# Three sections of the adaLN modulation moved from layer 0's route into its attention, and the FFN columns with them

## The chip, the core and the metric

The kernel runs on one core of a Trainium2 chip. The metric is device microseconds (us) of one execution, as the median of several. Engines are named as the profile names them: PE (TensorE; its weight loads are listed apart as PEld), DVE (VectorE), ACT (ScalarE), POOL (GpSimd) and SP (SyncE, which only issues transfers here).

## The reference, cut to what matters

A backbone of two layers over 256 latent tokens and 256 context tokens, 1024 wide, in float32. Each layer scales and shifts its inputs by vectors that come from a conditioning vector:

```python
for l in range(DEPTH):
    mod = (silu_c @ w_mod[l] + b_mod[l])[:, None, :]      # (1024) @ (1024, 6144)
    modc = silu_cc @ w_mod[l] + b_mod[l]
    sh_a, sc_a, gt_a, sh_f, sc_f, gt_f = jnp.split(mod, 6, axis=-1)
    h = modln(x, g_attn[l], sh_a, sc_a)                   # rmsnorm * (1 + scale) + shift
    y, yc = token_mixers(h, hc, ...)                      # conv, neighbourhood, window attention
    x = x + gt_a * y
    h2 = modln(x, g_ffn[l], sh_f, sc_f)
    yt = hier_moe(toks, ...)                              # 32 experts, top 1 group, top 2 experts
    x = x + gt_f * yt
return rmsnorm(x, g_final)
```

The six parts of `mod` are called sections here, numbered 0 to 5 in that order: (l, 0) and (l, 1) shift and scale the attention's input, (l, 2) is its gate, (l, 3) and (l, 4) shift and scale the FFN's input, (l, 5) is the FFN's gate. None of them depends on the tokens, so each may be computed at any time before its use. Layer 1 leaves out the context tokens' outputs.

## The kernel before, in words

The program is written out by hand for each engine, with semaphores between them; the order of an engine's instructions is the order of its function calls. The stages of a layer are: input projection, attention, gates and branches, output projection with the residual, then what I call the **route** (FFN norm, router, top-2 choice, ranks of the tokens in their experts, selection matrices), then the experts in 16 pairs.

**Weights** stream through a ring of six slots of 1 MB. SP issues them in the order of `weight_stream` (L120 to L150); a transfer is issued when the chunk six places ahead of it has been released by its reader. A few chunks go around the ring into spare buffers (`load_spare`, L699).

**A section of the modulation** is four chunks of 1 MB in that stream (`mod`, L947). A chunk is eight matmuls of 32x256 in fp32 on PE, which the profile shows as 16 records. After the fourth chunk DVE adds the bias (`mod_add`, L1882), and for section 4 applies the norm's scale. Until that is done, the next section may not write the same PSUM bank, 7; the sections of the route have banks of their own (`ROUTE_BANK`).

**FFN columns** (`ffn_columns`, L976): 64 tiny matmuls of 32x2 (two sections, 32 each) turn sections 4 and 3 into per-partition columns, in banks 6 and 7; DVE copies them to `f_mul` and `f_add` (L1967). They are needed where the turned tokens leave PSUM, in the FFN norm.

**Attention** (`attention`, L1136 on PE, L2046 on DVE) goes over steps, one head for two blocks of 128 queries: 12 steps on latent queries, and in layer 0 another 12 on context queries. In the loop's turn s, PE does, if s is odd, the latent scores of step s+1 and the attend of steps s-3 and s-2 (L1132), then always the transposes of step s-1 (L1117), if s is odd the context scores of s+1 (L1102), and at last the chunks of the modulation that belong to step s-1 (`mod_chunks`). DVE adds the bias table to the scores (L2064), copies transposed probabilities (L2080), normalises (L2088) and finds the maximum (L2095); ACT does the exponentials (L1645) and the other copies.

Layer 0 computes three sections there, (0,2), (0,4), (0,3), one chunk in every second step, and layer 1 its own three in the same order, one chunk in each step. The route of layer 0 holds (0,5) ahead of the FFN columns, (1,1) ahead of the ranks and (1,0) behind them; the route of layer 1 holds (1,5).

**Route on PE** (L1497 to L1517): (l,5), FFN columns, `turn_h` (L960, transposes of the normalised tokens, tile by tile as DVE and ACT have scaled them at L1974 and L1557), `route` (router matmuls L1215, L1221), in layer 0 `turn_rows` (L1226, the tokens turned back for the selection matmuls; ACT copies them out twice, L1733), `ranks` (L1236, waits for DVE's choice at L2200), and `first_x` (L1309 to L1327), which gathers the tokens of the first experts and waits for DVE's selection matrix (L2239). Then the first expert pair's gate and up products start (L1263).

## Time and profile before

| | us |
|---|---|
| median of 3 runs | 1362.85 |
| lowest, highest | 1360.55, 1365.0 |
| profiled execution, its own time | 1366.03 |
| its span, first to last instruction | 1364.2 |
| PE busy | 1226.1 (90% of the span) |
| DVE busy | 649.0 (48%) |
| ACT busy | 438.0 (32%) |
| mean granted TensorE clock | 0.966 |

All durations below are from the profiled execution, whose own time is 3.2 us above the median of the runs. In the rows of the trace a line reads: start, duration (both us), engine, line of the program, operation, what it writes and reads, number of records, and in brackets how long the engine was idle before it and what ended that. "issue" there means that the engine waited for nothing that the profile shows. A row of the stretches reads: from and to, length, then busy time and number of records of PE, PEld, DVE, ACT and POOL, the granted TensorE clock (1.00 is 2.4 GHz, 0.50 is 1.2 GHz), the share of time in which the DMA engines were busy, and GB/s. A row of the chain reads: start, duration, engine and line, number of records.

### The profile page before, as it was taken

The numbers are of one execution on the slowest core, as the hardware profiler recorded it, in microseconds if no ns is written. First come the engines' busy times: TensorE is split into PE (matmuls) and PEld (weight loads), VectorE is DVE, ScalarE is ACT, GpSimd is POOL, SyncE is SP. The second block draws the span as 40 slices with busy tenths as digits, with TensorE's granted clock in tenths as the row PEclk, the third lists the DMA queues.
The fourth block names the chain that finished last, engine by engine and source line by source line (L and its number), as shares of the span: only waits on it lengthen the run. The fifth ranks groups of instructions, "written<-read, shape, count | busy, mean of one in ns | idle before, by whom it ended". The sixth has DMA issues, their size and how long they took to land.

```text
span 1364.2 us, 22180 instructions
## 1 busy us (share of the span) xinstructions
PE 1226.1 (90%) x8966; PEld 936.5 (69%) x8966; DVE 649.0 (48%) x1503; ACT 438.0 (32%) x1041; POOL 171.6 (13%) x212
## 2 busy tenths in 40 slices
PE   4999888899998989899999789998998868889986
PEld 2788754688887966666666469965998755555652
DVE  1544586464345463422221285667776545233334
ACT  3533366433334350010000364356665510000001
POOL 1810000111011300100000401001111200000001
PEclk9899899999999999999999889999998879999998
DMA  9994145423323279999999985248555859999995
GB/s 353 314 351 151 62 142 192 131 93 93 93 93 124 93 276 417 360 411 414 416 386 373 385 206 155 93 154 264 180 183 188 322 214 419 419 415 415 388 373 185
DMA packets 131831, 351.14 MB, mean 257 GB/s; under 512 B 23054, under 2 KB 84726, under 8 KB 108561
## 3 DMA queue, kind: packets, MB, share of 16 engines
q1 hardware_dynamic: 118144, 317.69, 63.1%
q0 software_dynamic: 12304, 30.37, 6.6%
q10 hardware_dynamic: 1280, 1.66, 0.4%
q8 instruction: 73, 1.20, 0.4%
q14 instruction: 30, 0.24, 0.1%
HBM read 330.53 MB, written 28.86 MB: 263 GB/s over the span
## 4 chain that ended last, share of the span: by engine, by line
PE 80%; DVE 8%; issue 4%; DMA 4%; ACT 2%; POOL 0%; SPq 0%; DVEq 0%; ACTq 0%; POOLq 0%
PE banks L1021 33%; PE banks L1263 16%; PE banks L1277 8%; PE banks L1255 6%; PE banks L1189 4%; PE banks L958 3%; PE banks L1117 2%; PE banks L1132 2%; PE banks L1102 2%; DMA expert_rows<-arena,rows_u 1%; DMA ring<-in_w_in 1%; DMA ring<-in_w_mod 1%; DMA ring<-in_w_e_up 1%; DVE arena L2352 1%; DVE att L2080 1%
## 5 line engine op out<-in xcount | busy, mean ns | idle before, releaser
L1994 DVE TENSOR_TENSOR w_lo_r<-ring,w_hi_r 128x256 fp32r<-128x256 f32 x480 | 222.7, 474 | 241.2 <-ACT w_hi_r L1618 240.1
L1618 ACT ACTIVATE w_hi_r<-ring 128x256 fp32r<-128x256 f32 x480 | 197.4, 416 | 304.6 <-PE banks L1021 254.9
L1263 PE MATMUL banks<-ring,arena 128*64 128x256 f32 x2016 | 233.8, 385 | 28.1 <-issue 11.5
L1021 PE MATMUL banks<-h_hi_r,w_hi_r 128*128 128x512 f32 (+1 forms) x640 | 221.8, 347 | 6.1 <-DVE h_lo_r L1938 4.7
L1263 PEld LDWEIGHTS banks<-ring,arena 128*64 128x64 f32 x2016 | 162.5, 138 | 89.0 <-issue 37.4
L1021 PE MATMUL banks<-h_lo_r,w_hi_r 128*128 128x512 f32 (+1 forms) x640 | 220.2, 344 | 0.0
L1021 PE MATMUL banks<-h_hi_r,w_lo_r 128*128 128x512 f32 (+1 forms) x640 | 220.1, 344 | 0.0
L1021 PEld LDWEIGHTS banks<-h_hi_r,w_hi_r 128*128 128x128 f32 x640 | 122.9, 192 | 22.5 <-ACT arena L1588 4.8
L1021 PEld LDWEIGHTS banks<-h_lo_r,w_hi_r 128*128 128x128 f32 x640 | 123.0, 192 | 13.8
L1021 PEld LDWEIGHTS banks<-h_hi_r,w_lo_r 128*128 128x128 f32 x640 | 122.8, 192 | 13.8
L1277 PE MATMUL banks<-ring,att 128*64 128x512 f32 x424 | 119.3, 604 | 14.1 <-DVE att L2369 7.4
L1741 ACT ACTIVATE arena<-banks 128x256 f32<-128x256 f32 x32 | 12.3, 384 | 294.3 <-PE banks L1263 294.3
L1021 PE MATMUL banks<-w_hi_r,h_hi_r 128*128 128x256 f32 x320 | 94.7, 296 | 9.4 <-DVE w_lo_r L1994 9.1
L2362 DVE TENSOR_TENSOR arena<-arena,banks 128x256 f32<-128x256 f32 x32 | 13.5, 421 | 184.6 <-PE banks L1263 184.6
L1021 PE MATMUL banks<-w_hi_r,h_lo_r 128*128 128x256 f32 x320 | 92.8, 290 | 0.0
L1021 PE MATMUL banks<-w_lo_r,h_hi_r 128*128 128x256 f32 x320 | 92.7, 290 | 0.0
L1277 PEld LDWEIGHTS banks<-ring,att 128*64 128x64 f32 x424 | 36.9, 138 | 73.9 <-issue 71.4
L1255 PE MATMUL banks<-att_r,h_hi_r 128*128 128x256 f32 x336 | 85.5, 293 | 0.0
L898 POOL DMA_INDIRECT expert_rows<-arena,rows_u x30 | 29.5, 984 | 419.8 <-ACT arena L1750 166.7
L1255 PE MATMUL banks<-att_r,h_lo_r 128*128 128x256 f32 x336 | 81.3, 281 | 0.0
L1255 PEld LDWEIGHTS banks<-att_r,h_hi_r 128*128 128x128 f32 x336 | 63.4, 189 | 16.7 <-issue 16.7
L1021 PEld LDWEIGHTS banks<-w_hi_r,h_hi_r 128*128 128x128 f32 x320 | 63.6, 199 | 12.4 <-DVE w_lo_r L1994 11.2
(269 smaller groups left out, 1726.3 us busy)
## 6 DMA issues: line engine op xcount, KB each, us to landing
ring<-in_w_e_gate SPq DMA_DIRECT2D x64, 1024.0 KB, 8.7
ring<-in_w_e_up SPq DMA_DIRECT2D x62, 1024.0 KB, 9.3
ring<-in_w_e_down SPq DMA_DIRECT2D x53, 1024.0 KB, 9.3
ring<-in_w_mod SPq DMA_DIRECT2D x48, 1024.0 KB, 6.6
ring<-in_w_in SPq DMA_DIRECT2D x38, 1024.0 KB, 5.5
expert_rows<-att POOLq DMA_DIRECT2D x23, 512.0 KB, 20.3
ring<-in_w_o SPq DMA_DIRECT2D x8, 1024.0 KB, 5.1
ring<-in_w_branch SPq DMA_DIRECT2D x8, 640.0 KB, 4.5
```

The lines of the kernel that those rows point to most:

```text
L898: pool.indirect_dma_start(out=yd, out_offset=bass.IndirectOffsetOnAxis(ap=rows_u[:, p:p + 1], axis=0), in_=y_sb[n % 2], in_offset=None, bo ...
L958: ins = mm(banks[32 * q:32 * q + 32, mod_bank(l, sec), 0:CW], cond32[:, 2 * j2 + k, :], w[:, k, q * CW:(q + 1) * CW], start=j2 == 0 and k ...
L1021: ins = mm(out_ap, a, b, start=k == 0 and p_ == 0, stop=k == KD - 1 and p_ == 2)
L1102: ins = mm(banks[:, 2 * e + part, b * SEQ:(b + 1) * SEQ], arena[p0:p0 + HD, tn, q0 + b * P:q0 + (b + 1) * P], arena[p0:p0 + HD, kt, part * ...
L1117: ins = turn(banks[:, 4 + b, q * P:(q + 1) * P], S[s % 3][:, b, q * P:(q + 1) * P], ident)
L1132: ins = mm(banks[HD * e:HD * e + HD, O_BANK, 0:2 * P], vals[:, t0 + q, v0:v0 + HD], PT[e][:, q, :], start=q == 0, stop=q == n - 1)
L1189: ins = mm(outs[half], wt, y, start=k == BRANCH[b][0] and p_ == 0, stop=k == BRANCH[b][-1] and p_ == 2)
L1255: ins = mm(out, h[:, tt, k * P:(k + 1) * P], picked[:, tt, :], start=tt == 0 and h is th_hi, stop=tt == QT[l] - 1 and h is th_lo)
L1263: ins = mm(banks[e * CAP:(e + 1) * CAP, bank, 0:DE], x[:, k, e * CAP:(e + 1) * CAP], w[:, k * DE:(k + 1) * DE], start=k == 0, stop=k == KD ...
L1277: ins = mm(banks[e * CAP:(e + 1) * CAP, Y_BANK + half, :], rows[:, k, e * CAP:(e + 1) * CAP], w[k][:, half * 512:half * 512 + 512], start= ...
L1618: fn(w_hi[:, u % AHEAD, :, :], chunk(key)[:, q * KU:(q + 1) * KU, :], ACT.Copy).then_inc(w_hi_ready, 1)
L1994: v.tensor_tensor(w_lo[:, u % AHEAD, :, :], chunk(key)[:, q * KU:(q + 1) * KU, :], w_hi[:, u % AHEAD, :, :].bitcast(F32), ALU.subtract).th ...
```

## The change

All six sections that layer 0 used to compute from its attention on are computed in its attention: the order is (0,4), (0,3), (0,2), (0,5), (1,1), (1,0). `MOD_STEP` gives each chunk its step: one in each of steps 0 to 7, none in 8 and 9, two in step 10, then one in each step but for two in step 17. Layer 1 has (1,4), (1,3), (1,2) with chunks in steps 0 to 7, and two each in steps 9 and 10. In step 8 of either layer PE computes the FFN columns, into bank 7 beside the sections' 256 columns, and DVE copies them out in its turn for that step. Layer 1's (1,5) stays in the route, now in bank 7 and behind all of the residual's updates, not three quarters of them. The token tiles of `turn_rows` go to other banks, so that three tiles are turned ahead of the ranks, and one behind. The stream of weights follows the same order. The core of the diff:

```diff
@@ -114,3 +114,2 @@
-MOD_IN = [[(0, 2), (0, 4), (0, 3)], [(1, 2), (1, 4), (1, 3)]]
-MOD_ROUTE = [[(0, 5), (1, 1), (1, 0)], [(1, 5)]]
-MODS = [(0, 1), (0, 0)] + MOD_IN[0] + MOD_ROUTE[0] + MOD_IN[1] + MOD_ROUTE[1]
+MOD_IN = [[(0, 4), (0, 3), (0, 2), (0, 5), (1, 1), (1, 0)], [(1, 4), (1, 3), (1, 2)]]
+MODS = [(0, 1), (0, 0)] + MOD_IN[0] + MOD_IN[1] + [(1, 5)]
@@ -140 +139,2 @@
-        out += [("mod", k, 4 * sec + j) for k, sec in MOD_ROUTE[l] for j in range(4)]
+        if l:
+            out += [("mod", 1, 4 * 5 + j) for j in range(4)]
@@ -561,6 +561,4 @@
-        ROW_BANKS = [(3, 0), (4, 5), (3, 0), (4, 5)]
-        ROUTE_BANK = {(0, 5): 0, (1, 1): 7, (1, 0): 6, (1, 5): 0}
-
-        def mod_bank(l, sec):
-
-            return ROUTE_BANK.get((l, sec), MOD_BANK)
+        ROW_BANKS = [(3, 0), (4, 5), (6, 7), (3, 0)]
+        F_COL = {4: 256, 3: 256 + 2 * KD}
+        F_COL_STEP = [8, 8]
+        MOD_STEP = [[0, 1, 2, 3, 4, 5, 6, 7] + [10 + 14 * q // 16 for q in range(16)], list(range(8)) + [9, 9, 10, 10]]
@@ -570,2 +568 @@
-            n = 4 * len(MOD_IN[l])
-            return range(n * s // len(STEPS[l]), n * (s + 1) // len(STEPS[l]))
+            return [q for q, at in enumerate(MOD_STEP[l]) if at == s]
@@ -719 +716 @@
-                    sp.wait_ge(f_cols_done, 4)
+                    sp.wait_ge(f_cols_done, 2)
@@ -952 +949 @@
-                if n and j2 == 0 and (l, sec) not in ROUTE_BANK:
+                if n and j2 == 0:
@@ -953,0 +951,3 @@
+                for m in range(DEPTH):
+                    if j2 == 0 and (l, sec) == MOD_IN[m][2]:
+                        pe.wait_ge(f_col_ready, 2 * (m + 1))
@@ -958 +958 @@
-                        ins = mm(banks[32 * q:32 * q + 32, mod_bank(l, sec), 0:CW], cond32[:, 2 * j2 + k, :],
+                        ins = mm(banks[32 * q:32 * q + 32, MOD_BANK, 0:CW], cond32[:, 2 * j2 + k, :],
@@ -978,2 +978,2 @@
-                for sec, bank in ((4, 6), (3, 7)):
-                    pe.wait_ge(mod_out, MOD_AT[(l, sec)] + 1)
+                for sec in (4, 3):
+                    pe.wait_ge(mod_out, MOD_AT[MOD_IN[l][1]] + 1)
@@ -980,0 +981 @@
+                        at = F_COL[sec] + 2 * k
@@ -982 +983 @@
-                            ins = mm(banks[32 * j:32 * j + 32, bank, 2 * k:2 * k + 2], modr[:, l, sec, k::KD],
+                            ins = mm(banks[32 * j:32 * j + 32, MOD_BANK, at:at + 2], modr[:, l, sec, k::KD],
@@ -984 +985 @@
-                    ins.then_inc(f_cols_done, 1)
+                ins.then_inc(f_cols_done, 1)
@@ -1153,0 +1155,4 @@
+                        if s - 1 == F_COL_STEP[l]:
+                            ffn_columns(l)
+                pe.wait_ge(f_col_ready, 2 * (l + 1))
+                pe.wait_ge(mod_out, 2 + len(MOD_IN[0]) + l * len(MOD_IN[1]))
@@ -1228,2 +1233,2 @@
-                    if tt >= 2:
-                        pe.wait_ge(th_hi_ready, tt - 1)
+                    if tt == 3:
+                        pe.wait_ge(th_hi_ready, 1)
@@ -1314 +1319 @@
-                    pe.wait_ge(th_hi_ready, 3)
+                    pe.wait_ge(th_hi_ready, 4)
@@ -1317,3 +1321,0 @@
-                    for key in MOD_ROUTE[l][1:]:
-                        if k == ROUTE_BANK[key]:
-                            pe.wait_ge(mod_out, MOD_AT[key] + 1)
@@ -1497,3 +1498,0 @@
-                pe.wait_ge(upd_ready, 4 * QT0[l] + 3 * QT[l])
-                for j2 in range(4):
-                    mod(*MOD_ROUTE[l][0], j2)
@@ -1501,2 +1500,4 @@
-                ffn_columns(l)
-                pe.wait_ge(mod_out, MOD_AT[MOD_ROUTE[l][0]] + 1)
+                if l:
+                    for j2 in range(4):
+                        mod(1, 5, j2)
+                    pe.wait_ge(mod_out, MOD_AT[(1, 5)] + 1)
@@ -1506,4 +1507 @@
-                    turn_rows((0, 1))
-                for k, sec in MOD_ROUTE[l][1:2]:
-                    for j2 in range(4):
-                        mod(k, sec, j2)
+                    turn_rows((0, 1, 2))
@@ -1512,4 +1510 @@
-                    turn_rows((2, 3))
-                for k, sec in MOD_ROUTE[l][2:]:
-                    for j2 in range(4):
-                        mod(k, sec, j2)
+                    turn_rows((3,))
@@ -1889 +1884 @@
-                ins = v.tensor_tensor(dst, banks[:, mod_bank(l, sec), 0:CW], dst, ALU.add)
+                ins = v.tensor_tensor(dst, banks[:, MOD_BANK, 0:CW], dst, ALU.add)
@@ -1961 +1956,2 @@
-                mod_add(*MOD_ROUTE[l][0])
+                if l:
+                    mod_add(1, 5)
@@ -1964,5 +1959,0 @@
-                    if tt == nt // 2:
-                        for n, (dst, bank) in enumerate(((f_mul, 6), (f_add, 7))):
-                            dve.wait_ge(f_cols_done, 2 * l + n + 1)
-                            v.tensor_copy(dst[:, :, :], banks[:, bank, 0:2 * KD].rearrange("p (k s) -> p k s", s=2))\
-                                .then_inc(f_col_ready, 1)
@@ -2073,0 +2065,6 @@
+                        if s - 2 == F_COL_STEP[l]:
+                            dve.wait_ge(f_cols_done, l + 1)
+                            for sec, dst in ((4, f_mul), (3, f_add)):
+                                at = F_COL[sec]
+                                v.tensor_copy(dst[:, :, :], banks[:, MOD_BANK, at:at + 2 * KD].rearrange("p (k s) -> p k s", s=2))\
+                                    .then_inc(f_col_ready, 1)
@@ -2545,2 +2541,0 @@
-                if l == 0:
-                    mod_add(*MOD_ROUTE[0][1])
@@ -2549,3 +2544 @@
-                    rest_rows(0, range(2))
-                    mod_add(*MOD_ROUTE[0][2])
-                    rest_rows(0, range(2, 4))
+                    rest_rows(0, range(4))
```

How the order of the instructions changes, at three places on PE. In the rows, L1102 or L1103 are scores, L1117 or L1118 transposes of probabilities, L1132 or L1133 the attend matmuls, L958 a chunk of the modulation, L982 or L983 the FFN columns, L972 `turn_h`.

PE in layer 0's attention, turns 9 and 10 of the loop, before:

```order
L1117 MATMUL banks<-consts,att 128x128 [waits pt_act,pt_dve,p_ready]
L1117 MATMUL banks<-consts,att 128x128 x7
L1102 MATMUL banks<-arena 128x256 [waits s_act]
L1102 MATMUL banks<-arena 128x256 x3
L1117 MATMUL banks<-consts,att 128x128 [waits pt_act,pt_dve,p_ready]
L1117 MATMUL banks<-consts,att 128x128 x7
L958 MATMUL banks<-ring,cond 32x256 [waits loaded4,mod_out]
L958 MATMUL banks<-ring,cond 32x256 x7
```

and as changed:

```order
L1118 MATMUL banks<-consts,att 128x128 [waits pt_act,pt_dve,p_ready]
L1118 MATMUL banks<-consts,att 128x128 x7
L1103 MATMUL banks<-arena 128x256 [waits s_act]
L1103 MATMUL banks<-arena 128x256 x3
L983 MATMUL banks<-consts,modr 32x2 [waits mod_out]
L983 MATMUL banks<-consts,modr 32x2 x31
L983 MATMUL banks<-consts,modr 32x2 [waits mod_out]
L983 MATMUL banks<-consts,modr 32x2 x31
L1118 MATMUL banks<-consts,att 128x128 [waits pt_act,pt_dve,p_ready]
L1118 MATMUL banks<-consts,att 128x128 x7
```

The columns stand between the scores and the next transposes, and turn 10 has no chunk; two chunks follow in turn 11 and one in turn 12.

PE at the start of layer 0's route, before:

```order
L958 MATMUL banks<-ring,cond 32x256 [waits loaded5]
L958 MATMUL banks<-ring,cond 32x256 x7
L982 MATMUL banks<-consts,modr 32x2 [waits mod_out,upd_ready]
L982 MATMUL banks<-consts,modr 32x2 x31
L982 MATMUL banks<-consts,modr 32x2 [waits mod_out]
L982 MATMUL banks<-consts,modr 32x2 x31
L972 MATMUL banks<-consts,arena 128x128 [waits f_x_dve,f_x_act,f_col_ready,mod_out]
L972 MATMUL banks<-consts,arena 128x128 x7
```

and as changed, right behind the last matmul of the output projection:

```order
L1022 MATMUL banks<-w_lo_r,h_hi_r 128x256
L972 MATMUL banks<-consts,arena 128x128 [waits f_x_dve,f_x_act,f_col_ready,upd_ready]
L972 MATMUL banks<-consts,arena 128x128 x7
L972 MATMUL banks<-consts,arena 128x128 [waits f_x_act,f_x_dve]
L972 MATMUL banks<-consts,arena 128x128 x7
```

Nothing stands between the projection and `turn_h` any more; likewise the eight chunks around the ranks are gone.

PE at the start of layer 1's route as changed (before, it reads like layer 0's, with the four chunks first):

```order
L958 MATMUL banks<-ring,cond 32x256 [waits loaded5]
L958 MATMUL banks<-ring,cond 32x256 x7
L958 MATMUL banks<-ring,cond 32x256 [waits loaded0]
L958 MATMUL banks<-ring,cond 32x256 x7
L958 MATMUL banks<-ring,cond 32x256 [waits loaded1]
L958 MATMUL banks<-ring,cond 32x256 x7
L972 MATMUL banks<-consts,arena 128x128 [waits f_x_dve,f_x_act,f_col_ready,mod_out]
L972 MATMUL banks<-consts,arena 128x128 x7
```

The chunks stay, and the 64 matmuls of the columns no longer stand between them and `turn_h`.

## Rows read from the trace of the kernel before

**Rows 1.** The profile's page, parts 1, 3 and 4.

```profile
PE 1226.1 (90%) x8966; PEld 936.5 (69%) x8966; DVE 649.0 (48%) x1503; ACT 438.0 (32%) x1041; POOL 171.6 (13%) x212
...
q8 instruction: 73, 1.20, 0.4%
...
PE 80%; DVE 8%; issue 4%; DMA 4%; ACT 2%; POOL 0%; SPq 0%; DVEq 0%; ACTq 0%; POOLq 0%
```

**Rows 2.** Stretches: layer 0's attention, route and experts.

```profile
162.00:247.00 85.00, 69.47 (x602) 43.61 (x604) 65.28 (x160) 56.63 (x158) 2.49 (x4) 0.96 0.46 149
...
476.60:519.50 42.90, 37.52 (x500) 28.82 (x499) 26.71 (x92) 19.97 (x42) 3.68 (x6) 0.96 0.76 297
524.90:762.00 237.10, 223.46 (x1802) 153.38 (x1800) 59.53 (x158) 21.63 (x31) 20.15 (x23) 1.00 0.99 396
```

**Rows 3.** Chain of waits, attend matmuls: two of layer 0's, three of layer 1's.

```profile
188.48 1.95 PE banks L1132 x16
196.59 1.95 PE banks L1132 x16
...
916.12 1.95 PE banks L1132 x16
924.24 1.88 PE banks L1132 x16
932.91 1.95 PE banks L1132 x16
```

**Rows 4.** Timeline of PE in layer 0's attention, turn 12's transposes.

```profile
209.44 1.09 PE L1117 MATMUL banks<-consts,att 128*128 128x128 f32 x8 [0.77 <-DVE att L2088]
```

**Rows 5.** Timeline of layer 0's route, from the projection's end.

```profile
476.75 3.66 PE L958 MATMUL banks<-ring,cond 128*32 128x256 f32 x64
...
480.23 1.97 PE L982 MATMUL banks<-consts,modr 128*32 128x2 f32 x118
...
480.53 2.56 ACT L1557 ACTIVATE arena<-X,stat 128x512 f32<-128x512 f32 x4 [0.24 <-DVE stat L1960]
...
483.83 0.35 PE L982 MATMUL banks<-consts,modr 128*32 128x2 f32 x10 [1.64 <-issue]
...
484.49 3.81 PE L972 MATMUL banks<-consts,arena 128*128 128x128 f32 x32 [0.31 <-DVE f_add L1967]
```

**Rows 6.** Timeline of layer 0's route, from the choice to the first gather.

```profile
500.77 0.16 DVE L2202 TENSOR_TENSOR rt<-top_e 128x4 f32<-128x4 f32 x1
...
502.47 0.49 PE L1239 MATMUL banks<-att,consts 128*128 128x128 f32 x2
502.62 0.42 DVE L1889 TENSOR_TENSOR modr<-banks,modr 128x256 f32<-128x256 f32 x1 [1.68 <-PE banks L958]
...
507.79 1.67 DVE L2239 SCALAR_TENSOR_TENSOR att_r<-consts,sel_slot,att 128x256 fp32r<-128x256 f32 x4
...
509.74 4.02 PE L1323 MATMUL banks<-att_r,h_hi_r 128*128 128x256 f32 x32
```

**Rows 7.** Timeline of layer 1's route: the last update to `turn_h`.

```profile
1076.39 0.78 DVE L2156 TENSOR_TENSOR att<-banks,gate_t 128x256 f32<-128x256 f32 x2 [1.47 <-PE banks L1021]
...
1080.12 2.10 PE L982 MATMUL banks<-consts,modr 128*32 128x2 f32 x128
...
1080.71 0.73 DVE L1971 TENSOR_SCALAR arena<-X,stat 128x512 f32<-128x512 f32 x1
...
1082.56 1.21 PE L972 MATMUL banks<-consts,arena 128*128 128x128 f32 x8 [0.34 <-issue]
...
1088.04 1.97 PE L972 MATMUL banks<-consts,arena 128*128 128x128 f32 x8 [4.27 <-issue]
```

**Rows 8.** DMA queues from 1080 to 1088 us: packets, MB, share of time.

```profile
q8 instruction: 1, 0.02, 0.8%
```

**Rows 9.** Stretches: the first gathers of both layers.

```profile
509.70:517.50 7.80, 7.80 (x68) 7.57 (x64) 5.29 (x7) 1.01 (x1) 0.00 (x0) 1.00 1.01 415
...
1104.70:1110.30 5.60, 5.60 (x26) 5.60 (x27) 0.00 (x0) 0.00 (x0) 0.00 (x0) 0.50 0.09 34
```

## The prediction

> **What bounds the kernel now.** I read the profile's page first, then stretches by stage, then the chain of waits and the timeline where the change touches it. PE is busy for 90% of the span and holds 80% of the chain that ended last [rows 1]. Not so in each stage. In layer 0's attention PE is busy for 69.5 of 85 us and DVE for 65.3: neither is full, and the turns run at the pace of the chain between them [rows 2]. In layer 0's route PE is busy for 37.5 of 42.9 us, much of it with the modulation that is to move. In layer 0's experts the DMA engines are busy for 0.99 of the time at 396 GB/s [rows 2]: that stage starts when the first gate product can start, and its length is set by transfers behind it. So two things count: how much later attention ends, and how much earlier each layer's first gate product starts.
>
> 0.3%, or 4.1 us, is about what a measurement of this kernel can tell from no change.
>
> **Layer 0's attention, +3.0 us.** A chunk costs PE 3.66 / 4 = 0.92 us [rows 5]. Twelve more make 11.0 us, the columns 2.1 us: 13.1 us if nothing hid them. The trace has a direct comparison for the latent steps. Layer 0 has a chunk in every second step, and two steps take 196.59 - 188.48 = 8.11 us; layer 1 has one in every step, and two steps take 924.24 - 916.12 = 8.12 us [rows 3]. The second chunk is free there: PE fills a gap that it has ahead of the even turn's transposes, 0.77 us waiting for DVE [rows 4]. But where DVE does section 4's double addition, two steps of layer 1 take 932.91 - 924.24 = 8.67 us, 0.55 more [rows 3]. That addition moves from layer 0's light context steps into its latent ones: +0.5.
> The columns take 2.0 to 2.1 us of PE [rows 5, 7] in that gap of 0.77, so the next transposes come 1.3 us late; DVE has a copy to do for them and its own slack of some tenths: +0.9. It could be 0, or 2.1 and the stall of 1.64 that stands inside layer 0's columns now [rows 5], 3.7 in all.
> Step 10's two chunks are 1.83 us against 0.77: +1.1, bounds 0 and 1.8.
> In the context steps PE and DVE both have more room; of some seven added chunks I take +0.5, bounds 0 and 6.4 (none hidden).
> Sum +3.0, ends 0 and 13.1, both unlikely; +1 to +6 is what I keep. Twelve more transfers in this stage are 12.6 MB, 30 us at 415 GB/s [rows 9], on top of a share of 0.46 over 85 us [rows 2]: about 0.8, still free, and each is issued six chunks ahead. Cost nothing; if gates came late, the projection behind would show it. POOL now writes layer 1's gate row at the end of attention, ahead of its casts for the merge; these are first needed by the branch matmuls, behind three gate chunks, so nothing.
>
> **Layer 0's route, -1.5 us**, in three terms.
> The start: `turn_h` starts at 484.49, released by DVE's copy of the columns, whose matmuls stood still for 1.64 us [rows 5]. Without them it waits for the scaled tiles: ACT does four in 2.56 us from 480.53, so the first is there at 481.2 and the last at 483.1. At full clock the last tile is turned 0.95 us later, at 484.1, against 488.3 now: -4.2. But PE, which the modulation and the columns keep at work now, then stands idle from 476.6 to 481.2. Layer 1 shows what follows: after 4.27 us of idleness a tile takes 1.97 us, not 0.95 [rows 5, 7]. Four such from 481.2 end at 489.1: +0.8. I take the middle, -1.7, as the clock comes back within the stage.
> The ranks: the choice is ready at 500.93, but (1,1)'s chunks hold PE until 502.47, and its addition holds DVE for 0.42 us [rows 6]. Both go: -1.9. ACT's copies of the four tiles stay hidden, since three tiles are now turned ahead of the ranks.
> The first gather: it starts at 509.74, 0.28 us after the selection matrix (507.79 + 1.67), and takes 7.8 us at a clock of 1.00 [rows 6, 9], with (1,0) right ahead of it on PE. That work is gone; what is left is idle. Layer 1's gather, after idleness, runs 26 records in 5.6 us at 0.50, 0.215 us each; layer 0's 68 in 7.8, 0.115 each [rows 9]. If 4 to 5 us run so: +2.1; ends 0 and +7.8 (all of it at half rate).
> Sum -1.7 - 1.9 + 2.1 = -1.5; ends -6.1 and +6.7.
> What does not come back as time is the 12 MB: the ring holds six chunks, which in either order have landed before the first gate product. Layer 1 shows that state: 0.09 of DMA just ahead of it [rows 9].
>
> **Layer 1's attention, 0.** The columns come in (+0.9, bounds 0 and 3.7), and the last chunk and its addition leave the tail, where PE's 0.92 and DVE's 0.42 lie between the last transposes and the last attend (bounds 0 and -1.4): -0.9.
>
> **Layer 1's route, -5.5 us.** Tile 0 is turned at 1082.56, tile 1 only at 1088.04: PE stood still for 4.27 us with no wait that the profile shows, and the tile ends at 1090.0 [rows 7]. I put this down to PE running out of instructions. The instruction queue moved one packet in those 8 us, at a time when data transfers filled the engines [rows 8]. On the page 73 packets carry 1.20 MB, and PE's two rows count 17,932 instructions [rows 1]; if most packets are PE's, one holds about 250. The columns are 128 matmul records and as many weight loads, 256 in 2.1 us: they eat a whole packet while the next is on its way. Layer 0's columns show the same, 1.64 us [rows 5]. Moved into the attention, they no longer stand where the expert weights fill the queues.
> Then: (1,5) waits for the last update, at 1076.39 + 0.78 = 1077.2, takes 3.66 and ends at 1080.8; the addition ends near 1081.4; DVE's two scalings of 0.73 us make tile 1 ready near 1082.8 [rows 7]. Turned at 1.97 us it ends at 1084.9, at 0.95 at 1083.8, against 1090.0: -5.1 or -6.2. I take -5.5. If the stall stays, (1,5) later by some tenths and the columns gone leave about -1.2.
> By the Trainium skill, "Runtime: NRT & Kernel Launch", section "Instruction fetch mechanics", the next block is fetched while the current one is executed and crossing a block's end is mostly hidden; by that rule the 4.27 us would be something else and would stay, and the sum would be near 0. No row here decides between the two; the idle times behind both sets of columns speak for my reading.
>
> **Sum.** +3.0 - 1.5 + 0 - 5.5 = -4.0. Against the profiled execution that is 1366.0 - 4.0 = 1362.0; its own time lies 3.2 above the median, so against the median it is 1362.85 - 4.0 = 1358.8 us.
>
> **Rivals.**
> *The stall stays or moves.* The 4.27 us are not the columns', or they come back in the attention, which has the same 256 instructions in 2.1 us. For it: no row proves the cause. Against: two places, both at columns. -4.0 + 4.3 = +0.3: 1363.2 us. Chance 0.18, all but 0.02 of it within 0.3%.
> *Layer 0's route at half clock*, the slower side. The modulation was what kept PE at 2.4 GHz between DVE's pieces; without it `turn_h` ends 0.8 later, not 1.7 earlier (+2.5), and the whole gather runs at half rate (+7.8, not +2.1: +5.7), with 2 us in the router's matmuls. It decides once the idle stretches ahead of `turn_h` and of the gather, about 4.6 and 3 us, each bring the clock down, and it stays there, as over 5.6 us of layer 1's gather [rows 9]. -4.0 + 2.5 + 5.7 + 2 = +6.2: 1369.1 us. Against: in layer 0 PE has twice as much work in each burst. Chance 0.12.
> *More is won.* The clock holds in layer 0's route (-2.5 and -2.1), or the 12 MB that no longer queue there let the expert weights land sooner: -4.0 - 4.6 = -8.6, 1354.2 us. Chance 0.20.
> *The attention pays for the chunks in full* would be +13.1 and end slower too; rows 3 speak against it, and I fold it into the range.
>
> **How the numbers follow.** The forecast has 0.50, with a range of its own of 1355 to 1363; its centre lies at the bound of 0.3% (1358.8), so half of it is faster (0.26) and half within (0.24). With the rivals: faster 0.26 + 0.20 = 0.46, within 0.24 + 0.16 = 0.40, slower 0.12 + 0.02 = 0.14. For 8 in 10 the range must reach most of the way to the outer cases: 1351 to 1367.
>
> **What would show it.** In layer 1's route, `turn_h`'s second tile right behind the first, with no idle time of 4 us; the first gate product 5 to 6 us nearer to the end of the projection. In layer 0, `turn_h` some 4.6 us behind the last projection matmul, the ranks right behind DVE's choice, and a clock of 0.50 over part of the gather. In attention, latent pairs of steps still near 8.1 us but for those with section 4's addition, the columns and step 10. The prediction is wrong if layer 0's attention grows by more than 6 us, if an idle time of 2 us or more stands within or behind the columns in attention, or if the experts of layer 0 take another time than 237 us from their first gate product's end on.

## The result, and the profile after

The changed kernel takes 1387.17 us (median of 4 runs, 1378.04 to 1389.42) against 1361.70 us (4 runs, 1360.53 to 1365.00) on the same chip: a ratio of 1.017 with a 95% interval of 1.0121 to 1.022. The forecast was 1358.8 with a range up to 1367. The direction was wrong, and none of the rivals had this size.

The page of the changed kernel looks almost like [rows 1]: PE is as busy as before, with 15 us more of busy time.

```profile
PE 1241.2 (90%) x8966; PEld 946.5 (68%) x8966; DVE 648.7 (47%) x1503; ACT 439.2 (32%) x1041; POOL 171.7 (12%) x212
...
q8 instruction: 73, 1.20, 0.3%
```

The stretches that answer to [rows 2]: layer 0's attention, route and experts.

```profile
162.00:259.00 97.00, 85.49 (x926) 51.65 (x928) 65.85 (x164) 56.78 (x158) 2.32 (x4) 0.93 0.69 243
490.30:533.40 43.10, 30.29 (x176) 26.96 (x176) 25.12 (x86) 19.97 (x42) 3.36 (x6) 0.76 0.20 74
538.80:776.00 237.20, 222.46 (x1766) 153.24 (x1762) 59.31 (x156) 21.67 (x31) 20.09 (x23) 0.99 0.98 388
```

Attention is 12 us longer; PE has 16 us more work in it than before, and the granted clock is 0.93, not 0.96. The route lost 7 us of PE's work and not a microsecond of time: its clock went from 0.96 to 0.76.

Cut at the same events in each trace (us; the last column is a second profile of the unchanged kernel, the run `before_again`):

| from - to | before | after | difference | before again |
|---|---|---|---|---|
| start - layer 0's first attend | 172.37 | 172.30 | -0.07 | 172.83 |
| - its last attend | 74.43 | 86.19 | **+11.76** | 74.41 |
| - output projection's end | 230.02 | 231.78 | +1.76 | 228.53 |
| - first gate product (route) | 42.66 | 43.17 | +0.51 | 43.32 |
| - last down products (experts) | 254.24 | 257.24 | +3.00 | 259.91 |
| - layer 1's first attend | 134.20 | 134.35 | +0.15 | 132.73 |
| - its last attend | 41.03 | 48.38 | **+7.35** | 41.04 |
| - output projection's end | 127.76 | 128.51 | +0.75 | 126.83 |
| - ranks | 23.16 | 18.79 | **-4.37** | 22.06 |
| - end | 264.29 | 264.56 | +0.27 | 264.71 |

(The spans differ by 21.1 us, 1364.2 and 1385.3; the profiled run of before, at 1366.03, was 4.3 us above the median of its four runs, hence 25.5 between the medians.) The two attentions are the loss, 19.1 us. In the unchanged kernel their times repeat to 0.02 us from one profile to the next, while the experts' differ by 5.7 us; that stage keeps the DMA engines busy for 0.98 to 0.99 of the time, and its +3.00 says nothing about the change. In the changed kernel the attentions repeat less well. Four of the experiments below (`columns_repeated`, `long_products`, `kept_warm`, `warm_short`) leave its attention code as it is, and in these four profiles and its own layer 0's attention takes 86.2 to 88.9 us and layer 1's 46.6 to 48.5.

Inside layer 0's attention, from the timeline of PE and DVE:

```profile
199.18 1.09 PE L1118 MATMUL banks<-consts,att 128*128 128x128 f32 x8
201.27 1.90 PE L983 MATMUL banks<-consts,modr 128*32 128x2 f32 x108
203.93 0.54 PE L983 MATMUL banks<-consts,modr 128*32 128x2 f32 x20 [0.77 <-issue]
204.57 0.17 DVE L2069 COPY f_mul<-banks 128x16 f32<-128x16 f32 x1 [4.46 <-PE banks L983]
204.75 0.68 DVE L2077 COPY att<-banks 128x512 f32<-128x512 f32 x1
205.53 0.88 DVE L2085 TENSOR_SCALAR att<-att,rsum 128x512 f32<-128x512 f32 x2
206.47 1.97 PE L1118 MATMUL banks<-consts,att 128*128 128x128 f32 x8 [2.00 <-DVE att L2085]
...
223.81 0.42 DVE L1884 TENSOR_TENSOR modr<-banks,modr 128x256 f32<-128x256 f32 x1 [3.57 <-PE banks L958]
225.34 0.66 PE L1118 MATMUL banks<-consts,att 128*128 128x128 f32 x4 [1.67 <-DVE att L2085]
...
236.83 0.42 DVE L1884 TENSOR_TENSOR modr<-banks,modr 128x256 f32<-128x256 f32 x1 [2.70 <-PE banks L958]
```

This is what I did not see. DVE waits for the columns, or for a section's last chunk, at the head of a turn; the copy of P, the normalisation and the maximum stand behind that wait. The columns belong to step 8, so PE does them in turn 9. An odd turn is the full one: attend, transposes, scores, and only then the chunk. DVE stands for 4.46 us, its work comes late, PE waits 2.00 us for the normalised rows, and behind that the granted clock is 0.50: a turn's transposes take 1.97 us instead of 1.09. The last chunks of sections 2 and 5 fall on steps 12 and 16, also even, with idle times of 3.57 and 2.70. Before the change every section's last chunk stood at an odd step.

Layer 1's attention shows the same at its columns, with no stall inside them, and again in its last pair of steps, where section 2's last chunk falls on the even step 10:

```profile
954.00 2.15 PE L983 MATMUL banks<-consts,modr 128*32 128x2 f32 x128
956.29 0.17 DVE L2069 COPY f_mul<-banks 128x16 f32<-128x16 f32 x1 [3.45 <-PE banks L983]
958.19 1.97 PE L1118 MATMUL banks<-consts,att 128*128 128x128 f32 x8 [2.03 <-DVE att L2085]
...
968.59 0.42 DVE L1884 TENSOR_TENSOR modr<-banks,modr 128x256 f32<-128x256 f32 x1 [5.52 <-PE banks L958]
970.66 1.97 PE L1118 MATMUL banks<-consts,att 128*128 128x128 f32 x8 [2.13 <-DVE att L2085]
```

The routes. Layer 0's, then layer 1's (they answer to [rows 5, 6] and [rows 7]):

```profile
494.82 6.00 PE L972 MATMUL banks<-consts,arena 128*128 128x128 f32 x32 [4.55 <-ACT arena L1552]
...
513.50 0.80 PE L1244 MATMUL banks<-att,consts 128*128 128x128 f32 x2 [2.71 <-DVE att L2197]
...
521.08 6.61 PE L1325 MATMUL banks<-att_r,h_hi_r 128*128 128x256 f32 x32 [2.20 <-DVE att_r L2236]
...
1107.44 1.94 PE L972 MATMUL banks<-consts,arena 128*128 128x128 f32 x16 [1.34 <-ACT arena L1549]
```

In layer 0, `turn_h` begins 4.55 us behind the projection (forecast 4.6), but its 32 turns take 6.00 us instead of 3.81, and the gather's first half 6.61 instead of 4.02. In layer 1 the 16 turns run without the stall of 4.27 us. A slow `turn_h` is not new in itself: in the second profile of the unchanged kernel layer 0's takes 5.43 us, at no cost, since (1,1)'s chunks still stand between it and the ranks (18.05 us from its start to theirs, 17.98 in the first profile).

### The profile page after: what moved, and what is told of

Same layout as the page of the kernel before. It is cut to its first block and busy times, and to the rows that moved or that the text cites. A ratio compares the mean times of both kernels' runs of the same rounds, so it can differ in the third digit from the quotient of the medians.

```text
span 1385.3 us, 22186 instructions
## 1 busy us (share of the span) xinstructions
PE 1241.2 (90%) x8966; PEld 946.5 (68%) x8966; DVE 648.7 (47%) x1503; ACT 439.2 (32%) x1041; POOL 171.7 (12%) x212
## 5 line engine op out<-in xcount | busy, mean ns | idle before, releaser
L1268 PE MATMUL banks<-ring,arena 128*64 128x256 f32 x2016 | 237.9, 390 | 27.3 <-issue 10.6
L1260 PEld LDWEIGHTS banks<-att_r,h_hi_r 128*128 128x128 f32 x336 | 63.4, 189 | 16.7 <-issue 16.7
```

The lines of the kernel that those rows point to most:

```text
L1260: ins = mm(out, h[:, tt, k * P:(k + 1) * P], picked[:, tt, :], start=tt == 0 and h is th_hi, stop=tt == QT[l] - 1 and h is th_lo)
L1268: ins = mm(banks[e * CAP:(e + 1) * CAP, bank, 0:DE], x[:, k, e * CAP:(e + 1) * CAP], w[:, k * DE:(k + 1) * DE], start=k == 0, stop=k == KD ...
```

## The experiments

**Theory A**, formed from these traces: the place of DVE's wait, head of turn behind PE's full turn, costs the attention. **Theory B**, the rival: the chunks and columns are simply more work than PE's gaps hold.

### Four edits of the order

`columns_step_9`:

```diff
-F_COL_STEP = [8, 8]
-MOD_STEP = [..., list(range(8)) + [9, 9, 10, 10]]
+F_COL_STEP = [9, 9]
+MOD_STEP = [..., list(range(8)) + [10, 10, 11, 11]]
```

> The changed kernel with the FFN columns one step later, at the odd step 9 in both layers (layer 1's last section goes from steps 9, 9, 10, 10 to 10, 10, 11, 11, since it must come behind them). Theory A, the place of DVE's wait: at an even step PE does a chunk or the columns in its odd turn, behind attend, transposes and scores, and DVE waits for them at the head of its own turn with the copy of P, the normalisation and the maximum behind it; at an odd step PE does them right behind the transposes and DVE waits for little. Then the pair of steps with the columns falls from 12.4 us to about 9 and the next from 9.4 to about 8.5 in layer 0, and in layer 1 from 13.6 and 9.8 to about 9.5 and 8.3: 4 and 5 us less, 1387 to 1378. Theory B, PE's own work: 2.1 us of columns and the chunks are simply more than PE's gaps hold, wherever they stand, and an idle clock does the rest; then the pairs only trade places and the sum of each layer's attention stays within 2 us: 1385 to 1389.

`last_chunks_odd` (layer 0's chunks behind step 9):

```diff
-10 10 11 12 | 13 14 15 16 | 17 17 18 19 | 20 21 22 23
+10 10 11 13 | 14 15 16 17 | 18 18 19 19 | 20 21 22 23
```

> The changed kernel with layer 0's chunks behind step 9 on other steps, so that the last chunk of section 2 is at step 13 and that of section 5 at step 17, both odd (they were at 12 and 16); the columns stay at step 8 and the number of chunks is the same. Theory A (place of DVE's wait): the pairs of steps that cost 1.86 and 2.42 us more than before the change are back at 5.6 to 6.4 us, 4 us less in layer 0's attention, 1383 us. Theory B (the chunks' own time on PE): no change in the sum of the context pairs beyond 1 us, 1386 to 1388.

`columns_9_and_odd`: both, with 10, 11, 12, 13 for the first section.

> Both edits together, and step 10 with one chunk instead of two. Theory A: layer 0's attention ends 2 to 4 us later than before the change (it was 11.7), layer 1's takes 1 to 2 us more (it was 7.4), so 13 to 14 us less than the changed kernel, and some of the 1.9 us by which the projection behind attention grew and of the 2.8 us in layer 0's experts may go too: 1368 to 1374 us. Theory B: 1383 to 1388 us.

`adds_late` (DVE alone; `for_mod` holds the additions and column copies of step s - 2, as they were):

```diff
+def for_mod(l, s, late):
+    if s >= 2 and (s % 2 == 0) == late:
+        ...
 ...
-if s >= 2:
-    ...
+for_mod(l, s, False)
 if 0 <= s - 2 < n:
     ...
         v.tensor_reduce(negmax[:, s % 3, :], buf[:, :, 0:w], AX.X, ALU.max, negate=True).then_inc(max_ready, 1)
+for_mod(l, s, True)
```

> The changed kernel with PE's order untouched. Only DVE's waits and the work behind them (a section's addition, the two copies of the columns) that fall into its even turns, those for a chunk or columns of an even step, stand at the end of the turn, behind the copy of P, the normalisation and the maximum. The direct test of theory A: PE does the same work at the same places, so under theory B nothing changes (1386 to 1388). Under theory A the idle times of DVE of 4.46, 3.57 and 2.70 us ahead of the copy and the additions go, the pair with the columns falls from 12.4 to about 9.5 us, the context pairs by 1.5 to 2.4 us each, in layer 1 the pair of 13.6 to about 10: 10 to 13 us less, 1374 to 1377.

Measured, with the kernel before at 1362.77 us (19 runs) on the same chip: `columns_step_9` 1375.39 (5 runs), ratio 1.0081 (1.0049 to 1.0113); `last_chunks_odd` 1388.13 (4 runs), 1.0184 (1.0143 to 1.0225); `columns_9_and_odd` 1378.22 (9 runs), 1.0111 (1.0082 to 1.014); `adds_late` 1371.27 (10 runs), 1.0065 (1.0037 to 1.0093).

The distance from one attend to the next is the plainest measure, since each ends a pair of steps. It is worked out from the attends' starts in the timelines (us; pairs 4 to 11 are layer 0's, the last two layer 1's; the last three kernels come below; a last digit can be off by one through rounding):

| pair | before | after | step 9 | odd | late | columns_only | shifted | quarters |
|---|---|---|---|---|---|---|---|---|
| 4 | 8.05 | 12.38 | 9.02 | 13.09 | 9.18 | 8.96 | 8.30 | 8.06 |
| 5 | 7.09 | 9.38 | 9.49 | 9.37 | 10.19 | 8.66 | 9.88 | 7.54 |
| 6 | 6.44 | 8.30 | 8.30 | 6.44 | 6.44 | 6.44 | 6.44 | 6.98 |
| 7 | 6.20 | 5.58 | 5.57 | 5.57 | 5.57 | 5.58 | 6.27 | 5.58 |
| 8 | 5.58 | 8.00 | 8.00 | 6.27 | 6.33 | 5.58 | 5.58 | 5.58 |
| 9 | 5.58 | 6.27 | 6.27 | 8.00 | 6.28 | 5.58 | 5.58 | 5.58 |
| 10 | 5.58 | 5.58 | 5.59 | 5.58 | 5.59 | 5.75 | 6.74 | 6.21 |
| 11 | 5.68 | 5.68 | 5.67 | 7.37 | 6.73 | 5.09 | 5.09 | 5.09 |
| L1 columns | 8.05 | 13.62 | 9.02 | 12.64 | 8.94 | 8.30 | 8.30, 8.06 | 8.05, 8.06 |
| L1 last | 7.98 | 9.75 | 11.70 | 8.91 | 7.32 | 10.47 | 7.30 | 7.98 |

Theory A holds where it is tested alone. In `adds_late` PE's order is untouched and the pair with the columns goes from 12.38 to 9.18, the pairs of steps 12 and 16 from 8.30 and 8.00 to 6.44 and 6.33, layer 1's from 13.62 to 8.94. In its trace DVE's idle time ahead of the columns' copy is 0.96 us, not 4.46, and ahead of the additions of steps 12 and 16 there is none:

```profile
203.63 0.17 DVE L2041 COPY f_mul<-banks 128x16 f32<-128x16 f32 x1 [0.96 <-PE banks L983]
...
205.93 3.68 PE L1133 MATMUL banks<-att,arena 128*64 128x256 f32 x16 [0.84 <-DVE att L2080]
```

From the first attend to the last, layer 0's attention takes 81.31 us instead of 86.19 and layer 1's 41.26 instead of 48.38, both outside what the changed attention shows from one execution to another. The median, 1371.27, lies below the 1374 to 1377 of the forecast, 8.5 us above the kernel before on its chip, where the changed kernel stood 25.5 above; theory B had no change. The span is 16.7 us shorter, 12.0 of it in the two attentions; the rest is spread over the other stages.

Theory A is not all of layer 0's loss, though. Layer 1's attention is back at its old length (41.03), layer 0's is still 6.9 us above its 74.43. The largest part is pair 5, 3.1 us, which rose from 9.38 to 10.19 (7.09 before the change): its attend runs at half rate, 3.68 us instead of 1.95, and step 10's two chunks are in it. The pair with the columns keeps 1.1 us, three context pairs keep 0.7 to 1.1 each; one is 0.6 shorter than before the change.

`columns_step_9` also met its forecast at the columns (9.02); the pair behind them did not fall (9.49, forecast 8.5), and it lost some of the gain in layer 1's last pair (11.70), where four chunks had gone.

`last_chunks_odd` missed its 1383 us. The two pairs that it was made for fell as forecast (6.44, 6.27), and two others rose as much. The timeline of the pair that went from 6.27 to 8.00:

```profile
242.98 1.93 PE L958 MATMUL banks<-ring,cond 128*32 128x256 f32 x32
...
244.84 0.66 PE L1118 MATMUL banks<-consts,att 128*128 128x128 f32 x4
...
245.43 1.93 PE L958 MATMUL banks<-ring,cond 128*32 128x256 f32 x32
...
247.50 0.42 DVE L1884 TENSOR_TENSOR modr<-banks,modr 128x256 f32<-128x256 f32 x1 [3.03 <-PE banks L958]
```

The section now ends at step 19, odd, but with two chunks in each of two turns, and DVE waits 3.03 us for them. So an odd step is no rule in itself: here the wait is as long as all of PE's work up to the chunk that DVE waits for. The last pair (7.37) is another thing. DVE stands there behind a split of weights that ACT had to wait for:

```profile
258.65 1.33 ACT L1613 ACTIVATE w_hi_r<-ring 128x256 fp32r<-128x256 f32 x4 [1.99 <-DMA ring<-in_w_in]
259.10 1.43 DVE L1985 TENSOR_TENSOR w_lo_r<-ring,w_hi_r 128x256 fp32r<-128x256 f32 x4 [2.12 <-ACT w_hi_r L1613]
```

I read it as their ring slots coming free later, with the chunks; no run tests that alone. I had priced it at nothing.

`columns_9_and_odd` missed too, 1378 us for 1368 to 1374: the same two pairs rose (8.00 and 7.23), pair 5 stayed at 8.72 and layer 1's last at 10.39. Layer 1's pairs in `last_chunks_odd` (12.64 and 8.91) are no gain of its edit: `columns_repeated` and `long_products` have 12.66 and 8.91 with the changed kernel's attention.

### The stall in layer 1's route: instructions, or something else

Both edits stand in layer 1's route of the changed kernel, between section 5's chunks and `turn_h`.

`columns_repeated`:

```diff
+for sec in (4, 3):
+    for k in range(KD):
+        for j in range(4):
+            ins = mm(banks[32 * j:32 * j + 32, 5, 2 * k:2 * k + 2], modr[:, 1, sec, k::KD], ident[:, 32 * j:32 * j + 2], ...)
```

> The changed kernel with layer 1's 128 column matmuls done a second time in its route, behind section 5's chunks and ahead of turn_h, into a bank that nobody reads: the same number of PE instructions at the place where they stood before the change (the last spare load waits for them, as it did then). Theory C, PE runs out of instructions: a stall of 3 to 5 us with no wait that the profile shows comes back within or behind them, and the run is 5 to 7 us longer than the changed kernel's. Theory D, the stall of 4.27 us was something else that the change happened to remove: the repeated columns take their 2.0 to 2.1 us and turn_h follows without an idle time of over 1 us.

`long_products`:

```diff
+for _ in range(12):
+    ins = mm(banks[:, 5, 0:384], ident, consts[:, 0:384], ...)
```

> The control for the repeated columns: at the same place 12 products of 128x384 instead, which hold PE for about as long (by the rows with 512 columns, 0.23 us each, 12 x 0.17 = 2.05 us) with 12 matmuls and 12 weight loads at most instead of 256 instructions; the last spare load waits for them in the same way. Under theory C no idle time of over 1 us behind them; under D the same as the run with repeated columns. If both runs show the stall, it comes of PE's time or of the spare load's wait, not of the count.

The timelines of PE, first with the columns repeated, then with the long products:

```profile
1103.41 2.10 PE L1506 MATMUL banks<-consts,modr 128*32 128x2 f32 x128
1105.44 0.98 PE L972 MATMUL banks<-consts,arena 128*128 128x128 f32 x7
1109.22 2.08 PE L972 MATMUL banks<-consts,arena 128*128 128x128 f32 x9 [2.80 <-issue]
```

```profile
1108.78 8.01 PE L1504 MATMUL banks<-consts 128*128 128x384 f32 x24
1116.63 1.91 PE L972 MATMUL banks<-consts,arena 128*128 128x128 f32 x16
```

With the columns' 128 products and 128 weight loads done once more (records; the program has 64 of each) the stall is back, 2.80 us after the seventh turn; with few records there is none. Three flaws. The long products took 8.01 us, not 2.05, since each is two records of 0.33 us here, so this control is no equal in time. The stall came out a little under the 3 to 5 us expected. And the run's time, 1387.24 us (one run), is that of the changed kernel, not 5 to 7 us more: from the projection's end to the ranks layer 1 takes 21.73 us instead of 18.79, and other stages of this one execution were shorter by as much in sum. The second profile of the unchanged kernel shows how far the stall's size varies, at the same place (behind the eighth turn, where [rows 7] have 4.27):

```profile
1085.44 1.06 PE L972 MATMUL banks<-consts,arena 128*128 128x128 f32 x8 [0.34 <-issue]
1088.99 1.97 PE L972 MATMUL banks<-consts,arena 128*128 128x128 f32 x8 [2.48 <-issue]
```

The columns in attention bear it out. With the columns at step 8, six of seven traces have an idle time "issue" behind the same 108th record of layer 0's columns, 0.22 to 2.10 us long; with the columns at step 9, two of two have none. With the columns in halves at steps 8 and 9 (below), two of three have it behind the 100th (0.40 and 0.97), and `kept_warm` has 0.64 within layer 1's.

Counting settles the place. Put all of PE's entries in a trace in order of time, products, weight loads and semaphore instructions alike, and count those ahead of the first product behind the stall. They are 2753 in each of the eight traces with a stall in layer 0's attention, 5825 in layer 0's route in both profiles of the unchanged kernel, 12768 in layer 1's attention (`kept_warm`), 15072 in layer 1's route in both profiles of the unchanged kernel, and 15327 in `columns_repeated`. 2753 and 5825 lie 12 x 256 apart, 12768 and 15072 lie 9 x 256 apart, and 15327 is one short of another 256; between the two layers there is an offset of 31, for which I have no account. So all of these stalls stand where another 256 entries are through, which is what running out of instructions at the end of a block would look like; the fetch of a block is not itself in these rows. In `columns_step_9` number 2753 falls within the columns too, and nothing stops there: the 256 entries before it took 6.4 us, against 2.6 to 5.7 us ahead of all the stalls. A short block does not suffice for one: `shifted` passes such places after 5.7 and 3.2 us without a stall, `columns_repeated` one after 4.7.

The length is another matter. It does not follow the load of the DMA engines alone: they were busy for the whole of the stalls of 4.27, 2.48 and 2.80 us, and for 0.02 of the time in the one of 2.10 us (`long_products`, layer 0). The program decides the place; what decides the length is open.

### The cold clock in layer 0's route

`kept_warm` and `warm_short` put products that nobody reads into the gap ahead of layer 0's `turn_h`, 24 of them and 6:

```diff
+for _ in range(24):    # 6 in warm_short
+    mm(banks[:, 5, 0:384], ident, consts[:, 0:384], ...)
```

> The changed kernel with 24 products of 128x384 (24 x 0.17 = 4.1 us) in layer 0's route, behind the wait for the last update and ahead of turn_h, where PE stands idle for 4.55 us; what they compute is read by nobody. Theory E, the idle stretches that the change left in layer 0's route cost time by the clock: turn_h's 32 turns take 3.8 us instead of 6.0, the router and the choice come 1.5 to 2 us earlier, the gather is as slow as before since PE is idle again ahead of it: 1385 us against 1387. If the tiles or DVE set the pace of turn_h anyway, nothing changes (0 to +0.5 us).

> The changed kernel with 6 products of 128x384 in layer 0's gap of 4.55 us ahead of turn_h instead of 24. In the run with 24 they took 15.75 us, 0.66 each (two passes of 0.33), so 6 take 3.9 us and fit. Theory E (the clock that falls in the idle stretches left in the route costs time there): turn_h in 3.8 us instead of 6.0, the ranks 16.6 us behind turn_h's start as in the run with 24, instead of 18.7; 1.5 to 2 us less than the changed kernel, 1385. If the gain is lost again at the gather, which stays cold behind its own idle time, 0 to 1 us.

The 24 took 15.75 us instead of 4.1, by the same wrong price: 1391.83 us (ratio 1.0214, 1.0168 to 1.0261). The 6 fit into the gap: 1382.00 us, ratio 1.0149 (1.0127 to 1.0172), the kernel before at 1362.4 (17 runs). From the timeline of PE in `warm_short`:

```profile
488.40 4.14 PE L1506 MATMUL banks<-consts 128*128 128x384 f32 x12 [0.52 <-DVE att L2156]
492.44 3.81 PE L972 MATMUL banks<-consts,arena 128*128 128x128 f32 x32
...
508.86 0.49 PE L1244 MATMUL banks<-att,consts 128*128 128x128 f32 x2 [1.04 <-DVE att L2200]
...
515.37 6.41 PE L1325 MATMUL banks<-att_r,h_hi_r 128*128 128x256 f32 x32 [3.63 <-DVE att_r L2239]
```

`turn_h` is back at 3.81 us, the ranks' first products at 0.49 instead of 0.80, and the route at 39.6 us (527.50 - 487.88) instead of 43.17: 3.6 us from 4.1 us of work for nothing. The gather, behind an idle time of its own, stays at 6.41. This gain is read in the stage: `turn_h`'s start to the ranks is 18.4 to 18.8 us in the eight profiles with that gap left empty, 16.42 and 16.62 in the two with it filled. The ratios of the two kernels, 1.0149 and 1.017, do not differ clearly, their intervals overlap.

### The change cut down

`columns_only`: layer 0's sections go back to the route, the columns stay in attention, in halves at steps 8 and 9, DVE's even turns as in `adds_late`.

> Only the columns are moved: layer 0's three sections stay in its route, as in the kernel before, and each layer's columns stand in its attention, section 4's at step 8 and section 3's at step 9, with DVE's copies at turn 11; DVE's additions for even steps stand behind its maximum, and the sections' last chunks in the context steps are at odd steps. Theory A: layer 1's route is 4.7 us shorter, layer 0's 2 to 3, layer 0's attention 2 to 4 us longer (section 4's addition 0.6, the columns 1, half a clock behind them 1 to 2), layer 1's 2 to 3: 1357 to 1363 us, against 1362.8 before. Theory B (the attention pays for whatever is put there at its full price or more): 1366 us or more. If the 2.3 to 3.9 us by which layer 0's experts are longer in all runs with its sections in attention come of the sections, they are gone here; if of the columns, they stay.

1367.34 us (10 runs) against 1363.67 (13 runs), ratio 1.0034 (1.0009 to 1.0058): 4 us above the forecast range of 1357 to 1363 and in what the expectation had given to theory B (1366 or more), though its profiled span was 1362.7 against the 1364.2 and 1366.4 of the two profiles of before. The pairs show where: layer 1's last pair, with four chunks in its two steps, takes 10.47 us instead of 7.98. Layer 1's stretch to the ranks is 17.77 us (-5.4), layer 0's route 39.81 (-2.9) at a clock of 0.96; the attentions took 2.2 and 2.7 us more than before (first to last attend, 76.64 and 43.76).

`split_late` keeps all that the change moves, with the columns in halves, DVE's even turns late, and layer 0's chunks behind step 9 at 10 to 17 and 18 18 19 20 21 22 23 23:

> All that the changed kernel moves stays moved, but with its three faults taken out as the runs so far show them: DVE's additions of even steps behind its maximum, the columns in two halves at steps 8 and 9, never two chunks in a latent step of layer 0 and the last chunks at odd steps (13, 17, 20, 23). Theory A: layer 0's attention 3 to 6 us longer than before the change, layer 1's 3 to 4 (its last two steps carry four chunks), routes 5 us shorter, layer 0's experts 2.5 longer: 1366 to 1371 us, better than the changed kernel by 16 or more and still not better than the kernel before.

1375.89 us (4 runs), ratio 1.0101 (1.008 to 1.0122), above the forecast range. The last pair of layer 0, with three chunks in its two steps, took 8.85 us.

`shifted`, from `columns_only`:

```diff
-MOD_IN = [[(0, 4), (0, 3), (0, 2)], [(1, 4), (1, 3), (1, 2)]]
+MOD_IN = [[(0, 4), (0, 3), (0, 2), (1, 4)], [(1, 3), (1, 2)]]
-F_COL_AT: layer 1 at 8 and 9; its chunks at 0 to 7, 10 10 11 11
+F_COL_AT: layer 1 at 4 and 5; its chunks at 0 1 2 3, 6 7 8 9
```

> The kernel with only the columns moved, and layer 1's section 4 computed in layer 0's context steps (chunks at 12 to 15; section 2's layer 0 at 12 to 15, this one at 18 to 21), so that layer 1's attention carries two sections: chunks at steps 0 to 3 and 6 to 9, the columns in two halves at 4 and 5, none in the last two steps. Expected against the kernel with only the columns moved: layer 1's attention 2 to 3 us shorter (its last pair of steps 8.0 instead of 10.5, no double addition of 0.6), layer 0's 0.5 to 1.5 us longer in the context steps (a wait of 0.7 us per section, as the pair of 6.27 against 5.58 shows), 1 to 2 us less in all: 1364 to 1367 us by its 1367.3, level with the kernel before within 0.3%.

1360.93 us (12 runs) against 1362.4 (17 runs), ratio 0.9999 (0.9977 to 1.0021): no difference from the kernel before, and 3 us below the 1364 to 1367 expected. Layer 1's attention is down to 40.13 us, layer 0's is at 78.87. What was left there was above all pair 5, 9.88 us: the attend behind the columns ran at half rate.

`quarters` (from `shifted`), and `before_again`, the unchanged kernel:

```diff
-F_COL_AT[0] = {8: [(4, 0, KD)], 9: [(3, 0, KD)]}
+F_COL_AT[0] = {8: [(4, 0, 4)], 9: [(4, 4, KD)], 10: [(3, 0, 4)], 11: [(3, 4, KD)]}
+F_COL_AT[1]: the same at 4 to 7; layer 1's last section at 8 9 10 11
+layer 0's context chunks at 12 13 13 15, 17 18 19 21
```

> The shifted kernel with each layer's columns in quarters of 32 products, one behind each of four steps' turns (8 to 11 in layer 0, 4 to 7 in layer 1), the sections' last chunks in layer 0's context steps each behind a step without a chunk (chunks at 12, 13, 13, 15 and 17, 18, 19, 21), layer 1's last section at steps 8 to 11. If the clock falls behind the columns because 64 or more of these small products in a row leave PE little to do, the attend behind them runs at full rate again (1.95 us, not 3.68) and layer 0's pair of 9.88 us is back at 7.1 to 7.6; the context pairs of 6.27 and 6.74 are back at 5.6 to 5.8: 3 to 4 us less in layer 0's attention, 1357 to 1359 us, 0.3% better than the kernel before. If it is the idle time of 1.04 us ahead of the attend that brings the clock down, that pair stays above 9 us: 1359 to 1362.

> The kernel before, unchanged, for a second profile of it: the stage times on which the comparisons rest, from another execution. In eight profiles of changed kernels layer 0's experts take 2.3 to 7 us more from the first gate product to the last down product of the loop than the 254.2 us of the one profile of before. If that is the change, this profile shows 254.2 again within 0.5 us; if it is how its transfers happen to fall, it differs by 2 us or more. The attention's pairs of steps should agree within 0.1 us, the stall in layer 1's route (4.27 us) within 1.

In `shifted`, and in `quarters`, the attend that follows the last columns:

```profile
206.53 3.68 PE L1141 MATMUL banks<-att,arena 128*64 128x256 f32 x16 [1.04 <-DVE att L2095]
```

```profile
213.43 0.67 PE L990 MATMUL banks<-consts,modr 128*32 128x2 f32 x32
...
215.15 1.95 PE L1141 MATMUL banks<-att,arena 128*64 128x256 f32 x16 [1.04 <-DVE att L2095]
```

The idle time ahead of the attend is the same 1.04 us, and the attend takes 3.68 us in one and 1.95 in the other. So it is not that idle time alone: with the small products spread over four steps instead of two the clock held. Nor is it the small products alone. In layer 1 of `shifted` the same two runs of them are followed by scores in place of the idle time, and the attend takes 1.95 us:

```profile
922.67 1.17 PE L990 MATMUL banks<-consts,modr 128*32 128x2 f32 x64
923.77 1.13 PE L1111 MATMUL banks<-arena 64*128 64x256 f32 x8
924.88 1.95 PE L1141 MATMUL banks<-att,arena 128*64 128x256 f32 x16
```

In these rows it takes both. Pair 5 fell to 7.54, and layer 0's attention by 3.3 us as expected. The kernel as a whole did not reach the 1357 to 1359 us expected: 1361.69 us (12 runs) against 1364.03 (17 runs), ratio 0.9986 (0.9965 to 1.0008). The interval takes in no change, so I claim no version that beats the kernel before.

Of what the second profile of the unchanged kernel was to show, the experts differ by 5.7 us (259.91 and 254.24) and the pairs of steps agree within 0.02, as expected; the stall in layer 1's route differs by 1.8 us (2.48 and 4.27), more than the 1 expected.

## Why the prediction was wrong

**Layer 0's attention, "+3.0 us": measured +11.76.** The failed step is the columns' "+0.9 ... bounds 0 and 3.7" and, with it, the context steps' "+0.5". I counted what PE has to do against the gap that it has, and never asked where DVE waits for it. The columns' pair cost 4.3 us, the next 2.3 (step 10's two chunks, at +1.1, and the half clock), the sections ending at 12 and 16 cost 1.9 and 2.4; the context pairs together came to +4.4. With DVE's waits moved (`adds_late`) 4.9 of the 11.8 us go and the columns' pair costs 1.1 us, close to the +0.9. The 6.9 us that stay are the forecast's own terms, +3.0, two of them too small: step 10 with the half clock behind the columns 3.1 us for +1.1, the context pairs 1.9 for +0.5. Context pairs with one chunk in each step and no section's end took them for nothing (pairs 7 and 10, 5.58 us). The rest was right: section 4's addition 0.6 (forecast 0.5), latent chunks within 0.2 of free. My upper end, 13.1, was drawn as PE's full work and called unlikely (the terms' own upper bounds add up to 12.4); the real mechanism came close to it from another side. The prediction's own test, more than 6 us and an idle time of 2 us behind the columns, is what happened.

**Layer 1's attention, "0": measured +7.35.** The same step; "The columns come in (+0.9 ...)" was 5.6, above its bound of 3.7, and the last pair 1.8, where DVE waits 5.52 us at the head of its turn for section 2's last chunk and PE then 2.13 us for DVE. With late additions the two pairs are at 8.94 and 7.32, against 8.05 and 7.98 before: the columns cost 0.9 as forecast, and 0.7 of the tail's -0.9 was there to be had.

**Layer 0's route, "-1.5": measured +0.5.** The parts were right in kind. The router's products began 11.1 us behind the projection instead of 12.1 (forecast -1.7, measured -0.9). The gather, "+2.1", was 12.36 us from its start to the first gate product (533.44 - 521.08) against 9.74 before (519.48 - 509.74), so +2.6. The ranks' "-1.9" came out at -1.2 (501.41 to 521.08 is 19.67 us, before 20.85), since their own products ran at a clock of 0.50: from the ranks to the gather 7.58 us, in `warm_short` 6.51. `warm_short` shows what the clock cost here: 3.6 us, all but 0.2 of it ahead of the gather. The rival "half clock" had the mechanism at 0.12; it lay between it and the forecast.

**Layer 1's route, "-5.5": measured -4.4** to the ranks, and right in its cause as far as the runs go: the columns repeated bring the stall back, and the stalls stand where another 256 of PE's entries are through. `turn_h` itself ended 5.8 us nearer to the projection (7.46 instead of 13.30); 1.5 us of that were lost again before the ranks. Part of the size is luck of the one profile: in the second profile of the unchanged kernel the stall is 2.48 us and the stretch to the ranks 22.06, which leaves 3.3 us of gain. The Trainium skill, "Runtime: NRT & Kernel Launch", section "Instruction fetch mechanics", has it that crossing a block's end is mostly hidden by fetching ahead. The traces differ where PE's instructions are short: 2.5 to 4.3 us stood open in layer 1's route behind 256 records in 2.1 us, 1.6 and 1.9 us in layer 0's, and 0.2 to 2.1 us in attention. That the stall "comes back in the attention, which has the same 256 instructions" was my rival; it came back in part (0.77 us).

**The experts, "another time than 237 us" as a test of error:** a bad test. The stage varied by 5.7 us between two profiles of one kernel.

Taken together: the gain of the routes was a little over half of what was said (-3.9 against -7.0), and 19.1 us of loss in attention stood against +3.0.

## What to carry to other kernels

When work is moved into a pipeline of two engines, price not its time against a gap but the wait for it: find the instruction that consumes its result, ask what stands behind that wait in the same queue, and how much of the producer's work comes before the semaphore is raised. A consumer that isn't urgent goes to the end of its turn, behind what the next turn needs; with that alone the kernel stood 8.5 us above the one before, not 25.5. And work that leaves a stretch of small pieces may have been what kept the clock up there: price the stretch that stays at half rate too.

## What was not expected of the hardware

- Six products that nobody reads, 4.14 us in a gap of 4.55, shortened what followed by 3.6 us.
- With the same idle time of 1.04 us ahead of it, an attend took 3.68 us behind two runs of 64 of the columns' records and 1.95 behind four of 32; behind two runs of 64 without the idle time it took 1.95.
- The stalls of PE in and behind the columns stand at fixed numbers of its entries, multiples of 256 apart within a layer, in eleven traces.
- A product of 128x384 in f32 showed as two records and 0.66 us; 16 records of 128x512 in the experts took 3.65, which I had read as 16 products. It cost two runs their size.
- The unchanged kernel's attention repeats to 0.02 us, its experts to 5.7, and the changed kernel's attentions to 2.7 and 1.9: how far a single profile can be trusted has to be asked of each kernel and stage anew.
